# Squares of x taken in the first phase, next to the transposes, in place of a second load of x

## The reference

```
h = rms_norm(x, norm_g);  u, v, z = split(h @ w_in)          # layer A, w_in 2048 x 12288
y = gelu(u) * (tril(w_s) @ rms_norm(gelu(v)) + b_s) * silu(z);  x = x + y @ w_out
q, k, v, z, f = split(rms_norm(x, norm_g) @ w_in)             # layer B, w_in 2048 x 8208
y = attention(rms(q), rms(k), v, forget gates f) * silu(z);   x = x + y @ w_out
```

## Time and profile before

| | us |
|---|---|
| median of 3 executions | 2386.06 |
| lowest and highest | 2377.57, 2386.65 |
| the profiled execution | 2386.65 |
| its span in the trace | 2384.8 |
| TensorE busy | 2291.4 (96%) |
| VectorE busy | 1617.2 (68%) |
| ScalarE busy | 1065.6 (45%) |

### The profile page before, as it was taken

One profiled execution on the slowest core, in us unless ns is written; L12 is line 12 of the kernel. 1 busy time (PEld: TensorE's weight loads), 2 busy tenths in 40 slices (PEclk: granted clock), 3 DMA queues, 4 the chain that ended last, 5 costly groups with the idle time before them and its releaser, 6 DMA issues.

```text
span 2384.8 us, 26500 instructions
## 1 busy us (share of the span) xinstructions
PE 2291.4 (96%) x10413; PEld 1866.3 (78%) x10413; DVE 1617.2 (68%) x1676; ACT 1065.6 (45%) x1319; POOL 135.3 (6%) x185
## 2 busy tenths in 40 slices
PE   7999999999999999999999989999979999999999
PEld 5777788788887878878888877777767777778887
DVE  7778777877877777753222577776766877666665
ACT  5755545454544445452223444444443444344332
POOL 0011011000000000000000000100100000111000
PEclk9999999999999999999999999999999999999999
DMA  6678777776777677675344478885698897845333
GB/s 235 228 251 269 238 248 247 227 235 217 236 227 227 221 229 236 210 250 145 97 114 114 114 172 167 206 264 158 200 235 179 194 281 236 287 137 164 104 96 115
DMA packets 232892, 477.48 MB, mean 200 GB/s; under 512 B 19680, under 2 KB 26384, under 8 KB 231744
## 3 DMA queue, kind: packets, MB, share of 16 engines
q1 hardware_dynamic: 191056, 366.53, 54.7%
q0 software_dynamic: 18576, 67.28, 8.1%
q10 hardware_dynamic: 23136, 41.98, 4.7%
HBM read 393.90 MB, written 81.82 MB: 199 GB/s over the span
## 4 chain that ended last, share of the span: by engine, by line
PE 73%; DVE 10%; DMA 8%; issue 6%; ACT 1%; POOL 0%; SPq 0%; DVEq 0%; ACTq 0%; POOLq 0%
PE ps L1204 15%; PE ps L1206 15%; PE ps L1205 15%; PE ps L1362 5%; PE ps L1361 5%; PE ps L1363 5%; DVE u_lo L1651 4%; DMA t_rows<-t 4%; DMA raw<-in_b_w_in_dram 3%; PE ps L1584 2%; PE ps L1586 2%; PE ps L1585 2%; DVE raw L1636 2%; DMA raw<-t_rows 2%; PE ps L1507 2%
## 5 line engine op out<-in xcount | busy, mean ns | idle before, releaser
L719 ACT ACTIVATE u_hi<-raw 128x1536 fp32r<-128x1536 f32 (+1 forms) x320 | 544.7, 1702 | 820.0 <-PE ps L1206 783.2
L1651 DVE TENSOR_TENSOR u_lo<-raw,u_hi 128x1536 fp32r<-128x1536 f32 (+1 forms) x320 | 647.0, 2022 | 237.0 <-ACT u_hi L719 236.2
L1204 PE MATMUL ps<-u_hi,x1h 128*128 128x512 f32 x1280 | 514.5, 402 | 61.6 <-DVE u_lo L1651 55.4
L1205 PE MATMUL ps<-u_lo,x1h 128*128 128x512 f32 x1280 | 505.4, 395 | 0.0
L1206 PE MATMUL ps<-u_hi,x1l 128*128 128x512 f32 x1280 | 504.5, 394 | 0.0
L1204 PE MATMUL ps<-u_hi,x2h 128*128 128x512 f32 x960 | 381.7, 398 | 5.6 <-DVE u_lo L1651 4.9
L1206 PE MATMUL ps<-u_hi,x2l 128*128 128x512 f32 x960 | 375.6, 391 | 0.0
L1205 PE MATMUL ps<-u_lo,x2h 128*128 128x512 f32 x960 | 375.4, 391 | 0.0
L1204 PEld LDWEIGHTS ps<-u_hi,x1h 128*128 128x128 f32 x1280 | 244.1, 191 | 143.5 <-DVE u_lo L1651 79.3
L1206 PEld LDWEIGHTS ps<-u_hi,x1l 128*128 128x128 f32 x1280 | 244.1, 191 | 52.8
L1205 PEld LDWEIGHTS ps<-u_lo,x1h 128*128 128x128 f32 x1280 | 243.9, 191 | 48.2
(11 more groups left out here) (232 smaller groups left out, 2420.3 us busy)
## 6 DMA issues: line engine op xcount, KB each, us to landing
raw<-in_a_w_in_dram SPq DMA_DIRECT2D x280, 512.0 KB, 4.4
raw<-in_b_w_in_dram SPq DMA_DIRECT2D x184, 512.0 KB, 5.5
t_rows<-t ACTq DMA_DIRECT2D x160, 256.0 KB, 5.0
raw<-t_rows SPq DMA_DIRECT2D x160, 256.0 KB, 5.0
w_raw<-in_a_w_out_dram SPq DMA_DIRECT2D x128, 256.0 KB, 2.9
w_raw<-in_b_w_out_dram SPq DMA_DIRECT2D x64, 256.0 KB, 2.7
vz<-vz_rows POOLq DMA_DIRECT2D x16, 512.0 KB, 5.5
t<-yT_rows SPq DMA_DIRECT2D x28, 256.0 KB, 3.5
```

Of the source, the lines that this page charges most:

```text
L719: act.activation(u_hi[:, u_of(g), 0:n, :], raw_of(g)[:, 0:n, :], ACT.Copy).then_inc(hi1_ready, 1)
L1204: pe.matmul(dst[:, t, :], a, u_hi[:, s, pos, :], start=first, stop=False, skip_group_check=more)
L1205: pe.matmul(dst[:, t, :], a, u_lo[:, s, pos, :], start=False, stop=False, skip_group_check=more)
L1651: dve.tensor_tensor(u_lo[:, u_of(g), 0:n, :], raw_of(g)[:, 0:n, :], u_hi[:, u_of(g), 0:n, :].bitcast(F32), ALU.subtract).then_inc(lo1_read ...
```

## The change

The squares of chunk k are now taken right after `x_high1(k)`, while the chunk is in `stage`; the second load of five chunks is gone. `load_x(c)` waits for the squares of chunk c-3 besides its transpose. The scratch output of the squares lies elsewhere in SBUF. Around it, the order of ScalarE and VectorE in phase 0 is another: x is prepared two steps ahead of TensorE, where it was one. `x_stats_a` stands at step 4 of phase 1.

```diff
--- before.py
+++ after.py
@@ -108,7 +108,7 @@
         x2h = at("x2h", 65536, [P, KP, 3 * HF], F32R)
         x2l = at("x2l", 90112, [P, KP, 3 * HF], F32R)
         z2 = at("z2", 90112, [P, KP, 3, HF])
-        junk_x = at("junk_x", 188416, [P, NT, 2 * P])
+        junk_x = at("junk_x", 65536 + 18432, [P, NT, 2 * P])
         raw = at("raw", 114688, [P, 4, 4, FB])
         u_hi = at("u_hi", 147456, [P, 2, 4, FB], F32R)
         u_lo = at("u_lo", 163840, [P, 2, 4, FB], F32R)
@@ -419,14 +419,11 @@
 
         @block.sync
         def _(sp):
-            def load_x(n):
-
-                c = n % KP
-                if 3 <= n:
-                    sp.wait_ge(x_turned, min(n - 2, KP))
-                if n >= KP:
-                    sp.wait_ge(sq_ready, (n - KP + 1) * NT)
-                sp.dma_start(stage[:, n % 3, :, :], x_t[:, :, c * 2 * P:(c + 1) * 2 * P]).then_inc(x_loaded[n % 3], 16)
+            def load_x(c):
+                if c >= 3:
+                    sp.wait_ge(x_turned, c - 2)
+                    sp.wait_ge(sq_ready, (c - 2) * NT)
+                sp.dma_start(stage[:, c % 3, :, :], x_t[:, :, c * 2 * P:(c + 1) * 2 * P]).then_inc(x_loaded[c % 3], 16)
 
             def weights(u, row):
                 if u < VU:
@@ -495,8 +492,6 @@
                 load_step(0, 0, k)
             for k in range(KP):
                 load_step(0, 1, k)
-                if 2 <= k < 7:
-                    load_x(KP + k - 2)
             for u in range(1, NU):
                 for ph in range(2):
                     for k in range(KP):
@@ -758,19 +753,13 @@
                 act.activation(x2h[:, c, :].rearrange("p (s t) -> p s t", s=3), z2[:, c, :, :], ACT.Copy)\
                     .then_inc(x2h_ready, 1)
 
-            def x_square(i):
-
-                n = KP - 3 + i
-                c = n % KP
-                act.wait_ge(x_loaded[n % 3], (n // 3 + 1) * 16)
-                if i == 0:
-                    act.wait_ge(x1_ready, KP)
-                    act.wait_ge(s4_ready, KP)
-                else:
-                    act.wait_ge(sq_ready, i * NT)
+            def x_square(k):
+                act.wait_ge(x_loaded[k % 3], (k // 3 + 1) * 16)
+                if k > 0:
+                    act.wait_ge(sq_ready, k * NT)
                 for t in range(NT):
-                    act.activation(junk_x[:, t, :], stage[:, n % 3, t, :], ACT.Square,
-                                   accum_out=ssx8[:, t, c:c + 1]).then_inc(sq_ready, 1)
+                    act.activation(junk_x[:, t, :], stage[:, k % 3, t, :], ACT.Square,
+                                   accum_out=ssx8[:, t, k:k + 1]).then_inc(sq_ready, 1)
 
             def middle_leave(u):
                 (p1, *_), _, _, (p57, *_) = products_of(u)
@@ -796,8 +785,6 @@
             def end_leave(u):
 
                 act.wait_ge(m6_done, u + 1)
-                if u == 0:
-                    act.wait_ge(sq_ready, KP * NT)
                 if u > UB:
                     act.wait_ge(qkT_psum, turns_before(u + 1))
                     if stores_before(u + 1):
@@ -869,21 +856,24 @@
 
 
             act.wait_ge(cols_ready, 1)
-            x_leave(0)
-            x_high1(0)
-            high(0, 0, 0)
+            for k in range(2):
+                x_leave(k)
+                x_high1(k)
+                if k == 0:
+                    high(0, 0, 0)
+                x_square(k)
             for k in range(KP):
+                if k + 2 < KP:
+                    x_leave(k + 2)
                 if k + 1 < KP:
-                    x_leave(k + 1)
                     high(0, 0, k + 1)
                 else:
                     x_high2(0)
                     high(0, 1, 0)
                 store_t2(0, k)
-                if k + 1 < KP:
-                    x_high1(k + 1)
-                if k >= 6:
-                    x_square(k - 6)
+                if k + 2 < KP:
+                    x_high1(k + 2)
+                    x_square(k + 2)
             middle_leave(0)
             x_high2(1)
             x_high2(2)
@@ -891,8 +881,6 @@
                 high(0, 1, k)
                 if k + 2 < KP:
                     x_high2(k + 2)
-                if k < 7:
-                    x_square(k + 1)
 
             for u in range(1, NU):
                 for ph in range(2):
@@ -1771,19 +1759,21 @@
 
             dve.wait_ge(rows_T, 1)
             dve.tensor_copy(cols[:, :], ps[0][:, 0, 0:3 * KC]).then_inc(cols_ready, 1)
+            x_sums(0)
             sums(0, 0, 0)
+            x_sums(1)
             sum_t2(0, 0)
-            x_sums(0)
             for k in range(KP):
                 if k + 1 < KP:
                     sums(0, 0, k + 1)
-                    sum_t2(0, k + 1)
                 else:
                     sums(0, 1, 0)
                 low(0, 0, k)
                 if k + 1 < KP:
-                    x_sums(k + 1)
-                else:
+                    sum_t2(0, k + 1)
+                if k + 2 < KP:
+                    x_sums(k + 2)
+                elif k == KP - 1:
                     x_low2(0)
             for k in range(KP):
                 if k + 1 < KP:
@@ -1796,7 +1786,7 @@
                     x_low2(1)
                 if k + 2 < KP:
                     x_low2(k + 2)
-                if k == 7:
+                if k == 4:
                     x_stats_a()
             sum_t2(1, 0)
```

## The result

The changed kernel takes 2396.44 us (median of 6 executions, 2394.68 to 2402.56), the kernel before 2383.01 us on the same chip (median of 6, 2377.57 to 2386.65). The ratio is 1.0061, 95% interval 1.0046 to 1.0076: slower, by 11 to 18 us. A second set, taken with the last experiments, gives 1.0054 (1.0036 to 1.0071). The forecast, 10.9 us over the profiled execution before, is a ratio of 1.0046: it lies at the lower end of the first interval and inside the second. In us the forecast of 2397 looks closer than it was: the execution it was built on, 2386.65, is the slowest of the six, 3.6 us above their median. The profiled execution of the changed kernel took 2398.87 us, its span is 2397.0.

The account below looks back on a forecast made before the run. Phase 0 of unit 0 was taken to be bound by a two-step loop through TensorE, ScalarE and VectorE, phase 1 by TensorE; 8.4 + 3.9 - 1.2 - 0.2 = +10.9 us on 2386.65 gave 2397, range 2389 to 2403.

Parts of the forecast that it names:

- Part 1, the start: Start of phase 0, unit 0: the new order makes FH(0) 8.38 us later, at 25.33; counted as +8.4.
- the walk: Start of phase 0: new order followed link by link with old trace distances, from `x1l` at 12.09 to FH(0) at 25.33.
- Part 2, the loop: Phase 0: two-step loop through TensorE's transposes grows from 13.65 to 14.95 us, passed three times; +3.9.
- +0.97 for transposes and hand-over: Phase 0 loop: share of the 1.30 us growth per two steps put on waiting for TensorE's transposes and hand-over.
- I take 0.50 behind 3.0 too: Phase 0 even steps: 3.0 us idle gaps also followed by granted clock 0.50, as the old 1.83 us gaps were.
- the 14 that the forecast had named as a sign that it is wrong: Phase 0: forecast called wrong if the distance of the even steps is under 14 us.
- clock rivals: Phase 0: clock stays high, 2392.4 us (0.25 together with VectorE's pace), or more slow clock, 2401 to 2403 (0.17).
- Part 3: Phase 1: squares ahead of `middle_leave` go, SH(1) 1.17 us earlier against FH(7), -1.2; `x_stats_a` at step 4, -0.2.
- Part 4, transfers: Five dropped loads, 2.6 MB, lie beside a full TensorE; later loads have enough time: 0 us.
- not-slower rival: Phase 1: dropping 2.6 MB of loads frees DMA engines, 12 us back, time 2385.5; chance 0.05.
- VectorE's own pace: Phase 0: no loop, VectorE's 6.45 us a step against 6.83, time 2391; chance 0.25 together with clock high.

Follow-up runs that it names:

- e6: Changed kernel with VectorE doing `sums` and `t2` of step 0 before `x_sums(0)`, as in the kernel before; ratio 1.0051 to the kernel before.
- e2: Changed kernel without any squares of x, row factors made from constants; ratio 1.0049 to the kernel before.
- e1: Changed kernel with the old start, the order two ahead kept; ratio 1.0046 to the kernel before.
- a_again2: Changed kernel unchanged, profiled again; no ratio given, SH(0) at 75.38 us.
- b_again: Kernel before, unchanged, profiled again; ratio listed as 1, SH(0) at 66.77 us.
- e4: Changed kernel's squares and single load in the old order, one chunk ahead, with four more stage buffers; ratio 1.0010 to the kernel before.
- e5: As the changed kernel in work and loads, one ahead, `x_high1(k+1)` before `high(k+1)`, `sum_t2` behind `low`; ratio 1.0004 to the kernel before.
- e8: Kernel before, squares and second load kept, with `x_high1(k+1)` ahead of `high(k+1)` and `sum_t2` behind `low`; ratio 1.0002.
- e3: Kernel before, squares and second load kept, with only the changed ScalarE and VectorE order in phase 0 of unit 0; ratio 1.0046.
- e7: Changed kernel with the transposes of chunk k+3 behind the first of FH(k)'s three products; ratio 1.0049 to the kernel before.
- a_again1: Changed kernel unchanged, profiled and timed again; ratio 1.0054 to the kernel before.

## Why the prediction came out as it did

**Part 1, the start: right.** FH(0) was put at 25.33, 8.38 late; it came at 25.60, and counted from the first transposes 8.34 late (18.38 against 16.95 - 6.91 = 10.04). Of this, e6 shows 3.1 to be the late `sums` and `t2`, e2 1.6 the squares of chunk 0. The other 3.6 were not parted by themselves; in the walk they are `x_sums(1)` ahead of `low(0)`, and e1, which puts all of it back, has FH(0) at 16.63.

**Part 2, the loop: links right, clock not.** The links outside FH were put at 8.11 us and are 8.05, in each of the four passes shown. (In the forecast's account of the +1.30, "+0.97 for transposes and hand-over" should be 0.87, 6.84 - 6.07 + 0.10; the sum was made from the links and stands.) The loop's difference was put at +1.3 a pass with a slow stretch in each. In the profiled execution the passes took 15.15, 16.04 and 14.90, where 15.2, 14.95 and 14.95 were forecast, and FH(6) to the end of FH(7) took 11.08 (71.69 to 83.08 - 0.31) where 10.1 was. The step that failed is "I take 0.50 behind 3.0 too": the clock fell for longer in two places of that execution, and not at all in a_again2 behind the same gap. There the passes took 13.31 and 13.30, below the 14 that the forecast had named as a sign that it is wrong; the links held, so it is the clock that this sign caught. A slow stretch costs 1.6 of a step (6.85 against 5.25), not quite the 1.70 of the forecast. Both clock rivals occurred, each in some executions of one and the same kernel; they are not rivals but the spread of it.

My reading of the old loop was incomplete as well: with a full clock it is VectorE's pace that holds it at 12.97, so it gains only 0.7 a pass and not the 1.7 of the links. At full clock in both, the loop differs by 0.3 a pass from FH(2) on, and FH(6) is 10.5 us later (66.61 to 56.11, a_again2 and b_again); with slow stretches in both it is 13.5 (71.69 to 58.18). The marks at SH(0), 75.38 and 66.77, are not at equal clock: from FH(6) on it was 1.00 in a_again2 and 0.84 in b_again.

**Part 3: right.** In us from the start SH(1) was forecast at 86.5 and came at 88.75, late by what phase 0 was. It starts 5.98 behind the end of FH(7) (88.75 - 82.77), forecast 6.0. From there to TensorE's next wait, in unit 1, it is 45.84 us (to 134.59) against 45.93 (75.45 to 121.38): 0.1 gained, forecast 0.2. By e4, e5 and e8 the time of the whole program doesn't show 1 or 2 us.

**Part 4, transfers: right.** The DMA engines got freer, TensorE was as full as before (35.00 of 35.00 us), and the rest stayed at 2316 us, with and without the second load. The not-slower rival is refuted by that, and by e3. The rival "VectorE's own pace" falls with ScalarE's 4.20 us wait for the transposes, with VectorE's own wait of 2.44 behind it, and with e7.

**The sum.** +10.9 was forecast. The mean of SH(0) over four profiles after (79.7) less that over two before (67.8) is 11.9; from SH(0) to the wait in unit 1 the new order takes 1.0 less (51.51 against 52.54), which leaves 10.9. The two measured ratios say 13 and 14.5, with intervals from 8.6 to 18.

The central value was right by luck, an average over a clock that I had argued for as a certainty. The 2 to 4 us between the traces and the medians go at least in part with the clock as well. In the set of a_again1 the twelve timed executions of the changed kernel run from 2391.34 us at a mean granted clock of 0.993 to 2409.95 at 0.987. A straight line through the 32 executions of that set (14 of the changed kernel, 18 of the kernel before) gives 2.4 us per thousandth of clock, and at equal clock the changed kernel is 9.4 us slower, give or take 1.8 (two standard errors). The marks say nearly the same: 10.5 at FH(6) at full clock, less the 1.3 of part 3, is 9.2. That is a correlation and not an experiment, and how much of the rest's 8 us it explains stays open. No version here beats the kernel before.

## What to carry to other kernels

Before work is moved into a stage, walk the new order of each engine once from the first instruction, with the distances read from the old trace: an engine that was idle early can lose its head start to an order, and here that was most of the loss. Running one chunk further ahead helps only if what feeds it is moved too: with TensorE's order left alone, the weights of the next step waited behind a copy that had to wait for TensorE's transposes. And where a wait can be followed by a fall of the clock, price it as a range over executions, and compare kernels at equal clock.

## What the hardware did that I had not expected

Idle gaps of 3.0 us ahead of a step were followed by matmuls at 1.2 GHz in some executions and by full clock in others of the same kernel (0.76 and 1.00 for the stretch from 40 to 60 us), and in two of four executions FH(2) with its transposes took 8.0 us, 2.7 us more than at full clock. The first 4 to 11 matmuls of FH(0) start 0.43 us apart in the traces here, the pace of the slow stretches, though the clock column has 1.00 there (16.90 to 20.50 in the kernel before); what slows them isn't shown, and it keeps the first pass out of any comparison at full clock. The Trainium skill (TensorE: Matmul & The Clock Gate, What's actually happening) has activity lift a slow clock that is the default; the traces agree that the clock comes back while the step runs (FH(2) of the kernel before has 0.50 from 31.20 to 34.60, and behind it its matmuls start 0.23 us apart, against 0.43), but how long a gap was (1.83 us slow in the kernel before, 3.03 us fast in a_again2) did not tell whether it would fall.
